# Routed experts of a diffusion backbone: split fp32r products against plain fp32 products in four 32-column strips

## What is computed

```
C = max(1, EC_CAPACITY * N // N_EXPERTS)
aff = jax.nn.softmax((xs @ router_w).astype(jnp.float32), axis=-1)
gate, idx = lax.top_k(aff.T, C)
xe = xs[idx]
he = jax.nn.silu(jnp.einsum('ecd,edf->ecf', xe, w1)) * jnp.einsum('ecd,edf->ecf', xe, w3)
ye = jnp.einsum('ecf,efd->ecd', he, w2) * gate[..., None].astype(h.dtype)
out = jnp.zeros_like(xs).at[idx.reshape(-1)].add(ye.reshape(-1, D))
```

## Time and profile before

| | us |
|---|---|
| median of 3 runs (1925.4 to 1931.48) | 1926.5 |
| profiled execution, span | 1929.0 |
| one expert in the loop, start of one scatter to the next | 34.75 |
| experts of layer 0, first product to last | 415.7 to 978 |
| experts of layer 1, last product's end | 1906 |

### The profile page before, as it was taken

The page is one execution under the profiler, slowest core; times in us unless marked ns, Lnnn a source line. Parts: engine busy times, 40 slices in busy tenths (PEclk is TensorE's granted clock), DMA queues, the critical chain, the costliest instruction groups (busy, mean ns, idle before and its releaser), DMA issues.

```text
span 1929.0 us, 26934 instructions
## 1 busy us (share of the span) xinstructions
PE 1823.0 (95%) x9442; PEld 1276.1 (66%) x9442; DVE 1560.9 (81%) x2360; ACT 1156.5 (60%) x1549; POOL 311.8 (16%) x141
## 2 busy tenths in 40 slices
PE   4999988989999999999999999897999999999996
PEld 1776667856666666666667776685666666666663
DVE  4542767589999999999876367667999999999996
ACT  2410265358777778777652125624877777777773
POOL 0200031000322122221102003101032221222200
PEclk9999999989999999999999999998999999999998
DMA  9559201279999999999763722025999999999974
GB/s 343 183 182 322 95 39 45 99 286 420 397 400 379 385 378 376 386 387 374 286 209 134 262 67 88 16 106 215 421 403 386 383 384 386 379 374 384 382 299 159
DMA packets 86574, 540.02 MB, mean 280 GB/s; under 512 B 6929, under 2 KB 12051, under 8 KB 61925
## 3 DMA queue, kind: packets, MB, share of 16 engines
q1 hardware_dynamic: 76036, 502.54, 66.6%
q0 software_dynamic: 10464, 36.51, 6.9%
HBM read 515.50 MB, written 23.53 MB: 279 GB/s over the span
## 4 chain that ended last, share of the span: by engine, by line
PE 88%; DVE 7%; issue 2%; ACT 2%; DMA 1%; POOL 1%; SPq 0%; DVEq 0%; ACTq 0%
PE bank L1193 55%; PE bank L848 11%; PE bank L1035 5%; PE bank L724 2%; PE bank L1210 1%; PE bank L1203 1%; PE bank L1056 1%; PE bank L1073 1%; PE bank L994 1%; PE bank L979 1%; PE bank L883 1%; DVE arena_u L1915 1%; PE bank L1106 1%; PE bank L742 1%; PE bank L772 1%
## 5 line engine op out<-in xcount | busy, mean ns | idle before, releaser
L1499 ACT ACTIVATE arena_h_r<-ring 128x1024 fp32r<-128x1024 f32 x480 | 503.5, 1060 | 164.1 <-PE bank L1193 148.1
L2121 DVE TENSOR_TENSOR ring_r<-ring,arena_h_r 128x1024 fp32r<-128x1024 f32 x470 | 556.8, 1218 | 22.9 <-ACT arena_h_r L1499 16.0
L1193 PE MATMUL bank<-arena_h_r,arena_u_r 128*80 128x512 f32 x1280 | 373.3, 398 | 4.1 <-DVE arena_u_r L2159 4.1
L2121 DVE TENSOR_TENSOR ring_r<-ring,arena_u_r 128x1024 fp32r<-128x1024 f32 x282 | 333.4, 1219 | 12.7 <-ACT arena_u_r L1499 7.3
L1499 ACT ACTIVATE arena_u_r<-ring 128x1024 fp32r<-128x1024 f32 x288 | 300.8, 1059 | 58.9 <-PE bank L1193 58.9
L1193 PE MATMUL bank<-ring_r,arena_u_r 128*80 128x512 f32 x1024 | 318.8, 392 | 0.0
L1193 PEld LDWEIGHTS bank<-arena_h_r,arena_u_r 128*80 128x80 f32 x1280 | 188.6, 151 | 99.1 <-DVE arena_u_r L2159 4.5
L1193 PE MATMUL bank<-arena_u_r 128*80 128x512 f32 x768 | 216.9, 391 | 0.0
L1193 PEld LDWEIGHTS bank<-ring_r,arena_u_r 128*80 128x80 f32 x1024 | 152.2, 149 | 85.2 <-issue 1.4
L674 POOL DMA_INDIRECT arena_z<-xn_dram,icur x30 | 140.3, 4678 | 288.7 <-issue 274.9
L1193 PE MATMUL bank<-arena_h_r,arena_z_r 128*80 128x512 f32 x640 | 181.1, 397 | 3.6 <-DVE arena_z_r L2174 3.6
(11 more groups left out here) (319 smaller groups left out, 2608.0 us busy)
## 6 DMA issues: line engine op xcount, KB each, us to landing
ring<-in_exp_w SPq DMA_DIRECT2D x192, 2048.0 KB, 10.6
ring<-in_ada_w SPq DMA_DIRECT2D x24, 2048.0 KB, 8.6
ring<-in_w_in SPq DMA_DIRECT2D x8, 2048.0 KB, 18.2
ring<-in_w_out SPq DMA_DIRECT2D x2, 4096.0 KB, 12.7
x_res<-arena_z POOLq DMA_DIRECT2D x10, 512.0 KB, 3.7
xn_dram<-arena_u POOLq DMA_DIRECT2D x10, 512.0 KB, 2.9
arena_z<-x_res POOLq DMA_DIRECT2D x5, 512.0 KB, 4.2
arena_z<-in_x_sample SPq DMA_DIRECT2D x4, 512.0 KB, 6.4
```

Of the source, the lines that this page charges most:

```text
L1193: mm = pe.matmul(bank[out + n][0:CAP, :], xs[:, c, :], w[:, n * 512:(n + 1) * 512], start=(c == 0 and part == 0), stop=(c == KC - 1 and pa ...
L1499: act.activation(high[c], slot[s][:, c, :], ACT.Copy).then_inc(high_ready, 1)
L2121: v.tensor_tensor(slot_r[s][:, c, :], slot[s][:, c, :], high[c], ALU.subtract).then_inc(low_ready, 1)
```

## The change

All three weight products become plain fp32 matmuls in four column strips of 32. The 80 rows are padded to 96, three groups of 32. For `w1` and `w3`, strip q (PSUM partitions 32q to 32q+31) multiplies one group of rows with quarter q of the weight's columns, four strips on the same stationary rows; group 0, 1, 2 go to the two halves of one bank and the first half of the next. For `w2`, strips 0 to 2 hold the three groups with weight quarter g, and strip 3 holds group g with quarter 3. A product is 8 chunks x 3 groups x 4 strips = 96 matmuls of 256 columns. Nothing is rounded or subtracted any more: `rounded`, `rest`, the splits of the rows and of the hidden rows, and the `high` buffers are gone. PE's `hidden_T` is gone too: DVE writes the gated rows in an order in which one 128 x 768 transpose of 32 x 32 blocks turns them. The last quarter of the result's columns lies on partitions 96 to 127, so ACT moves it in three pieces (`moved`) before DVE multiplies it.

```diff
-        he = arena_z[0:CAP, 4096:5120]
-        heT = [arena_zr[:, a:a + KC * CAP].rearrange("p (c t) -> p c t", c=KC) for a in (5120, 5760)]
+        gated_h, hidden_q, heT = (arena_z[:, a:a + 3 * QUARTER] for a in (4096, 4864, 5632))
-                def product(m, s, out, x, between=(None, None)):
+                def products(m, s, e, out, x, between=(None, None)):
                     for c in range(KC):
...
+                            pe.wait_ge(half_in[s][c // HALF], (l * EXPERTS + e) * 16 + 16)
-                        parts = ((x[0], high[c]), (x[0], slot_r[s][:, c, :]), (x[1], high[c]))
-                        for part, (xs, w) in enumerate(parts):
-                            for n in range(2):
-                                mm = pe.matmul(bank[out + n][0:CAP, :], xs[:, c, :], w[:, n * 512:(n + 1) * 512],
-                                               start=(c == 0 and part == 0), stop=(c == KC - 1 and part == 2))
+                        for g in range(3):
+                            for q in range(4):
+                                if s == 2:
+                                    t, w = (q, g) if q < 3 else (g, q)
+                                else:
+                                    t, w = g, q
+                                mm = pe.matmul(group_out(out, g, slice(q * 32, q * 32 + 32)), x(c, t),
+                                               slot[s][:, c, w * QUARTER:(w + 1) * QUARTER],
+                                               start=(c == 0 and g % 2 == 0), stop=(c == KC - 1), skip_group_check=True)
                         mm.then_inc(chunk_used, 1)
...
-                        product(w1_next_at(e), 0, 0, xeT[1 - u], (3, lambda: hidden_T(e)))
+                        pe.wait_ge(silu, l * EXPERTS + e + 1)
+                        products(w1_next_at(e), 0, e + 1, 0, rows_of(1 - u))
...
+                def moved(e, u):
+                    act.wait_ge(chunk_used, AHEAD + chunks(l, w2_at(e), KC - 1))
+                    act.wait_ge(rows_free, l * EXPERTS + e + 1)
+                    y = ye_last if isinstance(e, int) and e == EXPERTS - 1 else ye[u]
+                    for g in range(3):
+                        n = min(32, CAP - g * 32)
+                        ins = act.activation(y[g * 32:g * 32 + n, 3 * QUARTER:D],
+                                             bank[4 + g // 2][96:96 + n, g % 2 * QUARTER:(g % 2 + 1) * QUARTER], ACT.Copy)
+                    ins.then_inc(y_moved, 1)
...
+                    v.wait_ge(he_done, l * EXPERTS + e + 1)
+                    v.transpose(heT, hidden_q).then_inc(heT_out, 1)
...
                 def expert(e, u):
-                    rest(w1_next_at(e), 0, {2: lambda: rows(e + 1, 1 - u), 3: lambda: rows_rest(e + 1, 1 - u)})
+                    rows(e + 1, 1 - u)
                     hidden(e)
-                    rest(w2_at(e), 2, {3: lambda: hidden_rest(e)})
-                    rest(w3_at(e + 1), 1)
                     result(e, u)
```

More of the change, by code:

```diff
@@ L1205, in rows_T @@
                     mm.then_inc(xeT_mm, 1)
[L1207 to L1212, removed]
                 def expert(e, u, k, last=False):
[L1216 to L1219, removed]
+                    products(w3_at(e), 1, e, 2, rows_of(u), (None, None) if last else (1, lambda: rows_T(1 - u, k + u)))
+                    if not last:
                         pe.wait_ge(xeT_out, l * (EXPERTS + 1) + e + 3)
-                        product(w1_next_at(e), 0, 0, xeT[1 - u], (3, lambda: hidden_T(e)))
+                        pe.wait_ge(silu, l * EXPERTS + e + 1)
+                        products(w1_next_at(e), 0, e + 1, 0, rows_of(1 - u))
                     pe.wait_ge(heT_out, l * EXPERTS + e + 1)
-                    product(w2_at(e), 2, 4, heT)
+                    products(w2_at(e), 2, e, 4, hidden_of)
                 pe.wait_ge(top_out, l + 1)
                 first_rows_T()
-                product(0, 0, 0, xeT[0])
+                products(0, 0, 0, 0, rows_of(0))
                 with pe.Fori(0, PAIRS - 1) as k:
@@ L1489, in _ @@
                 affinity(4, 5, bank[0])
[L1492 to L1513, removed]
@@ L1543, in _ @@
+                act.wait_ge(lg_mm, l * NT + NT)
+                act.wait_ge(chunk_used, AHEAD + chunks(l, 0, KC - 1))
+                act.activation(gated_h[:, 0:512], bank[0][:, :], ACT.Silu)
+                act.activation(gated_h[:, 512:768], bank[1][:, 0:QUARTER], ACT.Silu).then_inc(silu, 1)
                 gated(w1_next_at(0), 1)
[L1544 to L1547, removed]
+                moved(0, 0)
@@ L1548, in _ @@
+                with act.Fori(0, PAIRS - 1) as k:
                     for u in range(2):
[L1549 to L1552, removed]
+                        e = k * 2 + 1 + u
+                        gated(w1_next_at(e), e + 1)
+                        moved(e, 1 - u)
+                moved(EXPERTS - 1, 1)
             def final_root(n):
@@ L2196, in result @@
-                    ins.then_inc(ye_done, 1)
+                    y = ye_last if isinstance(e, int) and e == EXPERTS - 1 else ye[u]
+                    gate = gateT[:, bass.ds(e, 1)]
+                    for a, b, src in ((0, 512, bank[4][0:CAP, :]), (512, 768, bank[5][0:CAP, 0:QUARTER])):
+                        v.scalar_tensor_tensor(out=y[:, a:b], in0=src, scalar=gate, in1=gate2[:, a:b],
+                                               op0=ALU.mult, op1=ALU.mult)
+                    v.wait_ge(y_moved, l * EXPERTS + e + 1)
@@ L2218, in _ @@
-                rest(w3_at(0), 1)
-                rows(1, 1)
-                rest(w1_next_at(0), 0, {1: lambda: rows_rest(1, 1)})
-                hidden(0)
-                rest(w2_at(0), 2, {3: lambda: hidden_rest(0)})
-                rest(w3_at(1), 1)
-                result(0, 0)
-                expert(1, 1)
-                with v.Fori(1, PAIRS - 1) as k:
+                with v.Fori(0, PAIRS - 1) as k:
                     for u in range(2):
```

111 lines of the change are left out of this document (33 added, 78 removed).

## The result

The changed kernel takes 1998.05 us (median of four, 1992.81 to 1998.83), the kernel before beside it 1927.38 (1925.4 to 1931.48). The ratio is 1.0358, 95% interval 1.0338 to 1.0378: slower, where 1864.5 was forecast with a range that ended at 1904. The profiled execution has a span of 1991.0 us against 1929.0.

A forecast was written before the change was run, and what follows sets the result against it. PE was taken to set the pace, with the DMA stream close behind. 43.9 saved less 3 for meeting limits and 10 for jumps gave 31 us a layer, 62 in all: 1867 profiled, 1864.5 median, range 1836 to 1904.

The forecast's parts named there:

- PE's products: Expert products on PE: packs of four strips at 0.216 us, 32.1 us an expert, 2.65 less than now.
- The rival that PE can't be fed in strips: Expert products: if records sustain only 42 ns, a pack takes 0.34 us and the kernel 2416 us; chance 0.14.
- Per layer on PE: Each layer's PE work: 43.9 us saved, fifteen experts giving 39.8, experts from 415.7-978 to 415.1-934.
- Two limits that meet: Experts: PE and DMA limits both end at 934 us; their meeting costs 3 us a layer (0 to 10).
- The loop's code: Six jumps back per layer on PE: 2.5 us each for refetch, DMA regaining a third, 10 us a layer.
- The rule: PE instruction fetch, from the Trainium skill: 2048 instructions in blocks of 256; a taken branch to a block outside stalls.
- The 7 us that my forecast took as the most for a jump: PE's loop: the main forecast case had jumps costing 0.5 to 7 us, time 1845 to 1900; chance 0.58.
- The 11.8 us that I named as an upper bound: PE's loop jumps: the most a fetch could wait, taken from a gather's wait among full queues.
- The last expert: Layer's end: 2.0 us saved on the hidden rows' chain, 0.5 lost (0 to 1.5) to ACT's moves before the result.
- The sum again: Whole kernel: 43.9 - 3 - 10 = 31 us saved a layer, 62 in all, profiled 1929 to 1867.

The follow-up runs named there:

- with the weights out of the way: Written-out kernel with one chunk in four of each expert weight's half not loaded, from the second fill on; 1862.06 us.
- Without jumps: Changed kernel with PE's loop over pairs of experts written out, nothing else altered; 1889.65 us, ratio to the kernel before 0.9798.
- putting the result first: DVE's last result of layer 0 put ahead of the next layer's w_in low parts: written-out kernel 1880.12 us, changed kernel with its loop 1986.90 us.
- one body of 1644 instructions: Changed kernel, loop kept, six of eight w2 chunks and two of w3 left out but for one matmul each; one run, 1873.65 us.

## Why the prediction was wrong, point by point

**PE's products: right.** I took 0.216 us a pack and 32.1 us an expert. Measured: 0.216, the median of the packs, and 32.26. The rival that PE can't be fed in strips is refuted: 0.054 us a matmul record, each with its weight load, held for whole products. The Trainium skill, "TensorE: Matmul & The Clock Gate", section on the back-to-back issue gap, has about 81 ns a matmul for sustained pairs at 128 columns. As a lower bound it doesn't hold for the strips here, where a pair took 54 ns at 256 columns.

**Per layer on PE: 3 us too good.** 562.7 less my 43.9 are 518.8; with the weights out of the way 522.4 and 521.9 were needed. Some 2.4 of it is the 0.16 us that each of 15 experts takes more than my 32.1.

**Two limits that meet: mis-sized.** I took 3 us a layer, at most 10. Without jumps the experts took 535.8 and 537.1, 13 to 15 above PE's need and more than the 10 that I allowed. I had an expert at 32.9 us, from 13.24 MB at 403 GB/s; it took 33.7, with 13.5 MB at 400 GB/s (94.47 MB in the seven experts from 621.5 to 857.4 us, 0.52 of them PE's instructions, which my bytes left out; why the rest is more than 13.24 each stays open). This term didn't bear on the changed kernel itself, whose jumps let the transfers keep up (355 GB/s, 12.8 us to landing); there it counts 3 us too many.

**The loop's code: the step that failed.** The rule was known, the direction right and the place too: refetch at every jump. Its size was wrong. I took 2.5 us a jump, from the length of one packet, and of the 15 us a layer I gave a third back, which left 10. Measured are 10.6 us in the pass shown, 10.7 on average and 64.3 a layer, and nothing is given back, since PE and not the transfers was the limit. It has three parts, counted from the start of one pack to the start of the next, less the usual 0.216. The gap at the jump is 5.05 us: the 6.2 us from the jump to the first new pack, less 1.2 us of issued work. The gap where the body's first, short block runs out is 2.75 us in the pass shown, 2.2 to 3.8 in all. The third part is some 11 packs at 0.427 instead of 0.216 us with slower transposes, 2.8 us, because the clock was at 1.2 GHz. My sum had neither the second gap nor the clock. The 7 us that my forecast took as the most for a jump don't even cover the first two parts, 7.8 us. The 11.8 us that I named as an upper bound would have covered all three, but my range didn't use it. A jump's price was bounded by a queue's transfers; what stands behind a stop of PE was never costed.

**The last expert: half seen.** I put 0.5 us, at most 1.5, on ACT's moves before the last result. I counted what they add to that result and not what is queued behind them: the rounding of `w_in` on ACT, and behind it, through DVE's order, the result itself. Undoing it gained 9.5 and 11.2 us by the medians, 10.1 and 4.3 between the layers of the profiled executions.

**The sum again**, from the profiled spans: forecast 1867, measured 1991, 124 more. Jumps 2 x (64.3 - 10) = 108.6; PE's need 2 x 3.3 = 6.6; the limits that didn't meet, -6; between the layers 376.1 against 364.9, 11.2; a start 2.9 us later; the tail 0.3. That is 123.6. The start is scatter: it lies between 411.5 and 418.6 us over all the profiles, before and after the change alike. Of the 11.2 between the layers, putting the result first takes away 4.3 in the profile with the loop; 6.9 are left there, with the clock still low.

## What to carry to other kernels

Before a loop's body is lengthened on an engine, count its instructions, and the blocks that they touch, not only the work in them: here seven blocks of 256 cost 0.2 us a jump and eight cost 6 us and more, and writing the loop out turned 4% slower into 2% faster. Price a stop of PE with what comes behind it, the clock above all. And when a step is added to an engine, look for the first work that it pushes back and for whoever waits for that, up to an instruction that stands in the wrong place of a third engine's order.

## What was not expected of the hardware

- Where a body begins matters beside its length: 76 instructions ahead of it were worth 50 us over twelve jumps, and one body of 1644 instructions jumped in 0.21 us in one layer and in 6.3 to 7.2 in the other.
- The gap that a long jump leaves on PE depends on what was issued ahead of it: 2.3 us behind 512-column matmuls and 4.9 behind strips, for 6.2 and 6.0 us on the sequencer.
- In the pass shown the granted clock is at 1.2 GHz for 10 us around its two stops. After a wait of 8.5 us, 16 row sums took 14.02 us instead of 7.13; in the kernel with its loop and the result first they took 13.50 after a wait of only 1.8.
- 18,432 strip matmuls with as many weight loads ran at 0.054 us each, a quarter of 0.216.

Open is whether a loop with one expert in its body would do as well as the written-out form; that needs buffers chosen at run time and was not tried.
